# The second feed-forward block's down projection as seven block products, 256 tokens moving

## What is computed

```python
def swiglu_ffn(h, w_gu, w_down):
    g, u = jnp.split(h @ w_gu, 2, axis=-1)
    return (jax.nn.silu(g) * u) @ w_down
```

## Time and profile before

| what | value |
|---|---|
| median of three executions | 1921.63 us (1921.41 to 1921.93) |
| the profiled execution | 1922.35 us |
| its span (first to last instruction) | 1920.6 us |
| PE busy | 1910.1 us, 99% |
| DVE, ACT, POOL busy | 1390.4, 990.7, 351.4 us |
| second block: gate and up, first run | 739.95 to 830.66 us |
| its down projection, first half | 830.66 to 890.53 us |
| gate and up, second run | 890.53 to 1001.40 us |
| down projection, second half | 1001.40 to 1061.27 us |
| third block starts | 1061.27 us |
| fourth block's down projection | 1806.75 to 1915 us |

### The profile page before, as it was taken

One profiled execution on the slowest core, in us unless ns is written; L12 is line 12 of the kernel. 1 busy time (PEld: TensorE's weight loads), 2 busy tenths in 40 slices (PEclk: granted clock), 3 DMA queues, 4 the chain that ended last, 5 costly groups with the idle time before them and its releaser, 6 DMA issues.

```text
span 1920.6 us, 32099 instructions
## 1 busy us (share of the span) xinstructions
PE 1910.1 (99%) x11954; PEld 1728.2 (90%) x11954; DVE 1390.4 (72%) x2186; ACT 990.7 (52%) x1658; POOL 351.4 (18%) x349
## 2 busy tenths in 40 slices
PE   9999999999999999999999999999999999999998
PEld 7998998888898889989998999899898889999986
DVE  7865885677765658856875885687578558878887
ACT  7542554356564546533554553255356445555655
POOL 2200212100102212201211120021232113532020
PEclk9999999999999999999999999999999999999999
DMA  6744964323433637826953593496354336999695
GB/s 183 160 109 120 185 145 143 114 66 110 129 114 121 186 88 159 170 91 143 188 132 90 136 180 101 124 186 145 107 176 145 97 88 140 206 213 207 197 229 127
DMA packets 393689, 276.13 MB, mean 144 GB/s; under 512 B 19586, under 2 KB 370944, under 8 KB 393584
## 3 DMA queue, kind: packets, MB, share of 16 engines
q1 hardware_dynamic: 304464, 208.96, 36.8%
q0 software_dynamic: 80192, 63.78, 21.1%
q10 hardware_dynamic: 8928, 2.11, 0.5%
HBM read 264.31 MB, written 10.49 MB: 143 GB/s over the span
## 4 chain that ended last, share of the span: by engine, by line
PE 96%; DVE 2%; issue 1%; ACT 1%; DMA 0%; DVEq 0%; ACTq 0%
PE ps L458 17%; PE ps L459 17%; PE ps L460 17%; PE ps L1207 14%; PE ps L1206 14%; PE ps L1205 14%; PE ps L1102 2%; PE ps L1106 1%; PE ps L1104 1%; DVE w_lo L2331 1%; ACT w_hi L1588 0%; PE ps L1131 0%; DVE x L2807 0%; PE ps L1075 0%; DVE sums L3207 0%
## 5 line engine op out<-in xcount | busy, mean ns | idle before, releaser
L2331 DVE TENSOR_TENSOR w_lo<-raw,w_hi 128x512 fp32r<-128x512 f32 (+5 forms) x367 | 390.7, 1079 | 248.3 <-ACT w_hi L1588 248.0
L1588 ACT ACTIVATE w_hi<-raw 128x512 fp32r<-128x512 f32 (+5 forms) x367 | 337.2, 937 | 228.9 <-PE ps L460 182.0
L1205 PE MATMUL ps<-s_hi,w_hi 128*128 128x256 f32 x1248 | 353.2, 283 | 0.0
L1206 PE MATMUL ps<-s_lo,w_hi 128*128 128x256 f32 x1248 | 353.2, 283 | 0.0
L1207 PE MATMUL ps<-s_hi,w_lo 128*128 128x256 f32 x1248 | 353.2, 283 | 0.0
L1207 PE MATMUL ps<-h_hi,w_lo 128*128 128x256 f32 x936 | 264.9, 283 | 0.0
L1206 PE MATMUL ps<-h_lo,w_hi 128*128 128x256 f32 x936 | 264.9, 283 | 0.0
L1205 PE MATMUL ps<-h_hi,w_hi 128*128 128x256 f32 x936 | 264.9, 283 | 0.0
L1205 PEld LDWEIGHTS ps<-s_hi,w_hi 128*128 128x128 f32 x1248 | 239.6, 192 | 0.0
L1206 PEld LDWEIGHTS ps<-s_lo,w_hi 128*128 128x128 f32 x1248 | 239.6, 192 | 0.0
L1207 PEld LDWEIGHTS ps<-s_hi,w_lo 128*128 128x128 f32 x1248 | 239.6, 192 | 0.0
(11 more groups left out here) (436 smaller groups left out, 3873.7 us busy)
## 6 DMA issues: line engine op xcount, KB each, us to landing
raw<-in_ffn_w_gu SPq DMA_DIRECT2D x108, 512.0 KB, 4.7
raw<-in_ffn_w_down SPq DMA_DIRECT2D x24, 768.0 KB, 4.4
outer_even<-in_ffn_w_gu SPq DMA_DIRECT2D x70, 256.0 KB, 3.4
outer_even<-in_ffn_w_gu POOLq DMA_DIRECT2D x70, 256.0 KB, 6.8
raw<-in_ffn_w_gu SPq DMA_DIRECT2D x66, 256.0 KB, 5.9
raw<-in_x_w_kv SPq DMA_DIRECT2D x16, 1024.0 KB, 5.8
raw<-in_ffn_w_down SPq DMA_DIRECT2D x24, 640.0 KB, 4.2
outer_odd<-in_ffn_w_gu SPq DMA_DIRECT2D x58, 256.0 KB, 3.6
```

Source lines behind the costliest of these rows:

```text
L1205: nc.tensor.matmul(to, hi[:, kk, :], right_hi, start=fresh, stop=False, skip_group_check=True)
L1206: nc.tensor.matmul(to, hi[:, kk, :], right_lo, start=False, stop=False, skip_group_check=True)
L1588: return nc.scalar.activation(out_ap, in_ap, ACT.Copy, **kw)
L2331: return nc.vector.tensor_tensor(out_ap, value, hi.bitcast(F32), ALU.subtract)
```

## The change

`RUNS` becomes (2, 1, 2, 1): the second block has one run of 22 slots (20 mixed), its middle rows unsplit in `mid`, and its down projection is done with seven block products. Unlike in the fourth block, the weights stand still and 256 tokens move, and the output has features on the partitions, as x does. The engines' `down_products`, SP's loads and POOL's additions are the fourth block's functions with n as a parameter; token halves and column halves are exchanged for n = 1, so that chunks 0 to 3 of x are final after P7 and chunks 4 to 7 after P4, the last product. The wait before P3's weights stays for n = 3 alone. `feed_after_products` replaces `feed_last_pairs` of that block. The memory's columns are fetched by POOL after `add_down_sums(1)` (before: ahead of the second block's run), and `window_counts` moves from block 1 to block 2. Most other lines of the diff are counts of semaphores. Its core:

```diff
-    RUNS = (2, 2, 2, 1)
+    RUNS = (2, 1, 2, 1)
...
+            if f in AFTER_SEVEN:
+                n = AFTER_SEVEN[f]
+                return sig.evacuated, evacuated_after(n, P3 if m < KH else P7) + m % KH // 2 + 1
...
                 for g in range(3):
-                    sp.wait_ge(sig.w_lo_ready, SLOTS + tile(P2, min(2 * g + 1, PER - 1)) + 1)
-                    sp.wait_ge(CHAIN_ADDED[g][0], CHAIN_ADDED[g][1] + 32)
+                    sp.wait_ge(sig.w_lo_ready, w0 + tile(P2, min(2 * g + 1, PER - 1)) + 1)
+                    if n == 3:
+                        sp.wait_ge(CHAIN_ADDED[n][g][0], CHAIN_ADDED[n][g][1] + 32)
                     load_rows(P3, g)
...
-            pool.wait_ge(sig.part_done, at[("gu", 1, 0)].part)
+            add_run(1, 0)
+            add_down_sums(1)
             pool.dma_start(mem_cols[1][:], mem_scratch.rearrange("(c p) t -> p c t", p=P)).then_inc(sig.mem_loaded, 16)
-            add_run(1, 0)
-            add_run(1, 1)
             add_squares(4)
...
+            def down_by_column(n):
+
+                for k in range(LAST_TILE):
+                    i, q = DOWN_ORDER[k // PER], k % PER
+                    down_ready(n, k)
+                    hi, lo = down_w(n, w_hi, k), down_w(n, w_lo, k)
+                    right_hi, right_lo = down_forms(first_hi_forms, s_hi, k), down_forms(first_lo_forms, s_lo, k)
+                    nrows = DOWN_TILES[q][1]
+                    for c in range(C // 2):
+                        to, cs = ps[:, down_bank(n, i, c // 2), c % 2 * TH:(c % 2 + 1) * TH], slice(c * P, (c + 1) * P)
+                        for r in range(nrows):
+                            last = down_three(to, (hi[:, r, cs], lo[:, r, cs]), (right_hi[:, r, :], right_lo[:, r, :]),
...
@@ block.scalar @@
+            def feed_after_products(n):
+
+                f, w = FEED_AFTER[n], first_tile(n) + LAST_TILE
+                act.wait_ge(sig.w_lo_ready, w)
+                for m in range(KH):
+                    act.wait_ge(*x_final(f, m))
+                    feed_hi(f, m)
+                scale_x(f, 0)
+                feed_square(f, 0)
+                feed_square(f, 1)
+                split_hi(w % 2, area[w], loaded[w], slot_end[w - 3], C)
+                scale_x(f, 1)
+                feed_square(f, 2)
+                feed_square(f, 3)
+                for m in range(KH, C, 2):
+                    act.wait_ge(*x_final(f, m))
+                    for c in (m, m + 1):
+                        feed_hi(f, c)
+                    for c in (m, m + 1):
+                        feed_square(f, c)
+                scale_x(f, 2)
+                split_hi((w + 1) % 2, area[w + 1], loaded[w + 1], slot_end[w - 1], C)
+                scale_x(f, 3)
+                for kk in range(KH):
+                    x_sums_hi(f, kk)
...
@@ block.vector @@
+            def sum_x_last(f, kk):
+
+                low, sums = slice(0, TH), x_sums_early[:, kk]
+                dve.wait_ge(sig.x_sum_step, OPENED + 4 * KH * FEEDS.index(f) + 12)
+                nc.vector.scalar_tensor_tensor(sums[:, 3, :], x[:, kk + KH, low], gain(f, kk + KH), sums[:, 1, :],
+                                               ALU.mult, ALU.add).then_inc(sig.x_sum_step, 1)
...
+                def mid_scaled(s):
...
+                    nc.vector.tensor_tensor(mid[:, s, :], mid[:, s, :], rms[:], ALU.mult).then_inc(sig.mid_ready, 1)
+                    if s >= HALF:
...
+                        nc.vector.tensor_tensor(mid[:, s - HALF, second], mid[:, s - HALF, second], mid[:, s, second],
+                                                ALU.add).then_inc(ROW_SUMS[n][0], 1)
...
+            def feed_after_products(n):
+
+                f, w = FEED_AFTER[n], first_tile(n) + LAST_TILE
+                for m in range(KH):
+                    feed(f, m)
+                sum_x_first(f, 0)
+                split_lo(w % 2, area[w], w + 1, C)
+                sum_x_first(f, 1)
+                for j in range(2):
+                    take_product(n, P4, (j + 2,))
+                    feed(f, KH + 2 * j)
+                    feed(f, KH + 2 * j + 1)
+                first = mixed_slots.index(w + 2)
+                sum_x_first(f, 2)
+                split_lo((w + 1) % 2, area[w + 1], w + 2, C)
+                sum_columns(first)
+                sum_x_first(f, 3)
+                sum_three(first)
+                for kk in range(KH):
+                    sum_x_last(f, kk)
+                    x_sums_lo(f, kk)
+                sum_four(first)
```

More of the change, by code:

```diff
@@ L105, in place, with seven @@
             slot_rows.append(rows)
+    def seven(n):
+        return RUNS[n] == 1
     def run_slots(n, part):
@@ L124, in place_ffn @@
             if n == 3:
+                return
+            if seven(n):
+                for k in range(LAST_TILE):
+                    place(("tile", n, k), 2, sum(map(len, POSTS.values())) if k == 0 else 0, 1, loads=int(k < 6))
+                placed["plain"] += 1
                 return
@@ L204, in sum_count, with tiles_before, split_runs_before @@
         return OPENED + 3 * m - transfers_before(m) + step - int(by_transfer(m))
+    def tiles_before(m):
+        return LAST_TILE * sum(seven(n) and mixed_end(n, 0) <= m for n in range(3))
+    def split_runs_before(n):
+        return sum(not seven(i) for i in range(n))
     def tile(i, q):
@@ L209, in down_out, with down_part, first_tile, down_area @@
     def down_out(n, part):
-        return OUTS if n == 3 else at["down", n, part, 0, 0].out
+        if n == 3:
+            return OUTS
+        return at[("tile", n, 0) if seven(n) else ("down", n, part, 0, 0)].out
+    def down_part(n):
+        return PARTS if n == 3 else at["tile", n, 0].part
+    def first_tile(n):
+        return SLOTS if n == 3 else at["tile", n, 0].slot
+    def down_area(n):
+        return DOWN_AREA if n == 3 else area[first_tile(n)]
     def first_of_run(m):
@@ L1706, in mixed_run @@
                             form_hi(m + 1, i, sig.product_done, product_count(m, i))
-                    if not following and n < 3:
+                    if not following and not seven(n):
                         split_hi(w % 2, area[w], loaded[w], product_count(m, P6), slot_rows[w], sig.product_done)
@@ L1780, in ffn @@
                         w = at["down", n, part, pair, 1].slot
-                        if (n, part) == (1, 1) and pair >= 2:
-                            feed_last_pairs(f, pair, w)
-                        elif part == 1:
+                        if part == 1:
                             feed(f, 2 * pair)
@@ L2572, in mixed_run @@
                         low_gate(m, s)
-                    if not following and n == 3:
-                        down_form_lo(0)
+                    if not following and seven(n):
+                        down_form_lo(n, 0)
                     if following:
@@ new lines, in third_form @@
+            def third_form(n, q):
+                k0, nrows = DOWN_TILES[q]
+                ks, first, second = slice(k0, k0 + nrows), row_tokens(n, False), row_tokens(n, True)
+                other = slice(HALF + k0, HALF + k0 + nrows)
+                dve.wait_ge(sig.form_lo_ready, FORMS_DONE[n] + tile(P1, q) + 1)
+                dve.wait_ge(ROW_SUMS[n][0], ROW_SUMS[n][1] + HALF + q + 1)
+                nc.vector.tensor_tensor(mid[:, ks, first], mid[:, other, second], mid[:, ks, second], ALU.subtract)\
+                  .then_inc(ROW_SUMS[n][0], 1)
```

492 lines of the change are left out of this document (281 added, 211 removed).

## The result

The changed kernel takes 1931.5 us (median of 5 runs, 1930.65 to 1933.14) where the kernel before takes 1921.93 beside it (5 runs): ratio 1.0052, 95% interval 1.0039 to 1.0064. The forecast was 1930.1. The profiled execution of the changed kernel took 1933.14 us, span 1931.3; against the span of before, 1920.6, that is +10.7 us. Between the medians it is +9.6 us, and the interval lies wholly above 1.

A forecast was written before the change was run, and what follows sets the result against it. The prediction took PE, busy for 99% of the span, to bound the kernel. Products -8.9, weights +2.2, tail +13.2 and clock +2.0 summed to +8.5 us, 1930.1 us against the median; range 1923.5 to 1936.

The forecast's parts named there:

- The products: Second block's down projection: 924 matmuls at 120.0 ns replace 528 at 226.8 ns, a gain of 8.9 us.
- signs of being wrong: Token-scales wait under 5 us, products' stretch over 116 us, or matmuls after the wait keeping 226.8 ns.
- The weights: In the seven products, P5's weights come late behind accumulating transfers: 2.2 us of stalls, bounds 0 and 4.
- the first addition: First accumulating transfer into P5's weights, usable at about 30.6 us after the products' start; the second at 37.3.
- The tail: DVE work after the last product delays the third block's token scales: 13.2 us, bounds 9.4 and 15.
- Turns: In the tail, four strictly serial rounds of last step, ACT's split and DVE's lower part: 2.85 us each, 11.4 together.
- The clock: After the token-scales wait, half of 24 matmuls run at half speed: 2.0 us, bounds 0 and 5.4.
- the faster one: Rival: token scales in time at the third block's opening, -6.7 us, 1914.9 us; chance 0.07.
- the low bound of the tail: Rival near no change: POOL's additions fall into DVE's waits, tail 9.4 us, +2, 1923.6 us; chance 0.20.
- the starved additions: Rival: P3's early loads in the second block delay the accumulations, 2.2 becomes about 8, 1936 us; chance 0.08.

The follow-up runs named there:

- e1: The changed kernel with P3's weights in the second block also held until the second addition to w_chain has landed: 1926.93 us, ratio 1.0024.
- e7: The changed kernel with P3's weights held, last steps of the x sums issued together before their splits, and token scales' root and reciprocal ahead of both: 1917.94 us, ratio 0.9978.
- e4: The changed kernel with POOL's additions of squares for the third block's first norm cut to one column, only times being read: 1928.01 us, ratio 1.0032.

## Why the prediction was right

*The products.* The arithmetic came as forecast; it was not kept. The stretch lasted 116.40 us: 924 x 0.120 = 110.9, waits of 1.34 and 2.19 (from matmul to matmul), about 1.6 at half speed in P5, where some 15 matmuls of 256 columns were 0.21 us apart instead of 0.12, and 0.4 at the edges of the cut (0.3 of it stands in e1 and e7 too, which have no wait there). The prediction called itself wrong if this stretch lasted over 116; it did by 0.4. The forecast so met one of its own signs of being wrong, and the fault was in the next term.

*The weights* were the mis-sized term: 2.2 us forecast, 3.5 measured, plus the half speed. The place (P5, first and third tile) and the first addition (usable at 30.7 us after the start; forecast 30.6) were right; the second came at 38.7, not 37.3. The estimate took the accumulation at one rate for both; the second took 1.4 us longer. Bounds of 0 to 4 held the waits, not the half speed behind them (5.1 together). The sum had no term for the clock among the products: it put a fall only behind the one wait of some 9 us.

*The tail.* The reciprocal was forecast 30.4 us after the end and was done at 29.6; without POOL 26.6, and e4 gave 26.0. Turns of 2.85 were 2.74. The waits ahead were 1.05 at chunks 6 and 7 (forecast 1.5) and 2.0 at the second slot's weights (2.2). The wait at the token scales was forecast at 8 to 10 us and was 5.9 and 7.3: PE came late to it, since the half slot ahead of it had run at half speed for a part. That does not change the sum, for PE cannot go on before the reciprocal in either case: it goes on 12.4 us later than the 17.24 of before, forecast 13.2.

*The clock* in the opening: forecast 2.0, measured 2.2 and 2.4 in the 24 matmuls behind the long wait, 2.5 and 2.7 with the four small ones. The forecast had it that half of the 24 run at half speed; here 9 and 10 of them did, and the first was slow too, so the size was good, though it rested on a guess that no row of before could bear out. The opening as a whole: forecast 13.2 + 2.0 = 15.2, measured 12.4 + 2.5 = 14.9. The Trainium skill, page "TensorE: Matmul & The Clock Gate", section "What's actually happening", says that an array that was idle is passed the lower clock until it has been busy for a while. Before the change no row showed matmuls after such a fall, and now 13 of them stand 0.43 us apart behind the wait at the second slot's weights and 9 behind the wait for the token scales, and then again 0.23 apart: the trace agrees.

*The sum.* Products -3.2 (forecast -8.9 + 2.2 = -6.7), opening +14.9 (forecast +15.2), the rest of the kernel -1.1 (forecast 0): +10.7 between the spans, where +8.5 was forecast. The profiled execution was a long one; between the medians it is +9.6. That the forecast of +8.5 lies only 1.1 from this is partly luck: the products lost 3.5 more than forecast, while 0.3 in the opening and 1.1 behind it, which the sum had at 0, came back. The rivals: the scales came 12.4 us after the point at which PE could have taken them, so the faster one falls; the low bound of the tail (9.4) falls, since POOL held DVE as in the row before, for 3.6 us (e4); of the starved additions only a part came: the products lost 5.1 us, not 8, and behind P5 no wait followed.

## What to carry to other kernels

When a faster form of a stage ends it all at once instead of piece by piece, ask first what the next stage had been getting under its last piece: here 8.9 us of arithmetic were paid for with 12.4 us of small steps that had been hidden and 2.5 us of half clock behind the wait that they made. Then order these steps by who waits for them, and let two engines work through a list side by side (all of one's, then all of the other's) rather than hand each item to and fro. A load that is early can take bandwidth from an accumulating transfer that is wanted sooner; here holding it back was worth 5 us in one block and 3 in another.

## What was unexpected of the hardware

The granted clock fell behind waits as short as 2 us, in a PE that was full before and after them. Over all profiles of kernels with such waits: behind the pair of waits in P5 (0.7 to 2.5 us each) the clock fell in 6 of 8 profiles, behind the 2.0 us wait at the second slot's weights in 5 of 6, behind a pair of 2 and 1 us at the mixed slot in none of 2; behind a single wait of 4.1 to 8.7 us in 5 of 5. The half speed then lasted 3.4, 6.8 or 10.2 us, and the matmuls in it stood nearly twice as far apart (0.43 us instead of 0.227): behind the 2.0 us wait at the second slot, 13 of them each 0.2 us late, and a slow first one, lost another 2.9 us (8.45 us for the half slot, 5.54 at full speed). In the changed kernel a later wait hid this; in e7 nothing did, and 1.6 us of such a loss stayed. So such a wait can cost more than twice its length, and by an amount that differs from one execution of the same kernel to the next. Why it fell in some executions and not in others stays open.
